# Rows through TensorE as transposes, and probabilities scaled on GpSimd ahead of their transposes, in a fused two-block transformer kernel

## What is computed

```
s_loc = q @ k.T * dh ** -0.5, -inf outside |i - j| <= 128
s_ctx = q @ k_c.T * dh ** -0.5
m     = max(max(s_loc), max(s_ctx), s_sink)
denom = sum(exp(s_loc - m)) + sum(exp(s_ctx - m)) + exp(s_sink - m)
o     = (exp(s_loc - m) @ v + exp(s_ctx - m) @ v_c) / denom
```

## Time and profile before

| what | value |
|---|---|
| median of 3 runs | 1319.2 us (1318.8 to 1322.29) |
| profiled execution | 1322.93 us |
| its span | 1320.9 us |
| TensorE matmul, busy | 1286.4 us, 97% of the span |
| VectorE busy | 896.2 us, 68% |
| ScalarE busy | 580.9 us, 44% |
| GpSimd busy | 109.9 us, 8% |

### The profile page before, as it was taken

How to read it: one execution, slowest core, us unless ns; L and a number is a source line. 1 busy time by engine, 2 the same in 40 slices (tenths; PEclk the granted TensorE clock), 3 DMA queues, 4 the chain that set the end, 5 groups by cost and what they waited for, 6 DMA issues and landing times.

```text
span 1320.9 us, 24297 instructions
## 1 busy us (share of the span) xinstructions
PE 1286.4 (97%) x10377; PEld 1196.9 (91%) x10377; DVE 896.2 (68%) x1387; ACT 580.9 (44%) x908; POOL 109.9 (8%) x161
## 2 busy tenths in 40 slices
PE   6999999999999999999999999999999999999997
PEld 4899999999998788999998998998999899899997
DVE  4577755576474564668587786786888986767567
ACT  4533355644774453534413213213165664535431
POOL 0111110000001111000000011110000210000000
PEclk9999999999999999999999999999999999999999
DMA  9997896545245453222445455575435102545550
GB/s 355 386 305 240 263 247 168 144 149 184 72 161 173 147 189 128 82 83 90 154 156 160 143 171 186 177 242 165 145 98 192 33 1 92 195 160 189 182 173 33
DMA packets 170152, 218.39 MB, mean 165 GB/s; under 512 B 6158, under 2 KB 147861, under 8 KB 169910
## 3 DMA queue, kind: packets, MB, share of 16 engines
q1 hardware_dynamic: 140196, 148.11, 34.4%
q0 software_dynamic: 29152, 67.42, 16.8%
q10 hardware_dynamic: 698, 1.32, 0.3%
HBM read 215.70 MB, written 1.12 MB: 164 GB/s over the span
## 4 chain that ended last, share of the span: by engine, by line
PE 87%; DVE 6%; ACT 2%; issue 2%; DMA 1%; SPq 1%; POOL 0%; DVEq 0%; ACTq 0%
PE bank L1353 31%; PE bank L705 12%; PE bank L724 11%; PE bank L757 7%; PE bank L740 4%; PE bank L1257 2%; PE bank L816 2%; PE bank L1331 1%; PE bank L903 1%; PE bank L1016 1%; PE bank L1431 1%; PE bank L1448 1%; PE bank L1499 1%; PE bank L1181 1%; DVE wlo L2151 1%
## 5 line engine op out<-in xcount | busy, mean ns | idle before, releaser
L2151 DVE TENSOR_TENSOR wlo<-raw,whi 128x2048 fp32r<-128x2048 f32 x131 | 297.3, 2274 | 90.2 <-ACT whi L1542 89.5
L1542 ACT ACTIVATE whi<-raw 128x2048 fp32r<-128x2048 f32 x131 | 248.0, 1899 | 187.0 <-PE bank L1353 133.2
L1353 PE MATMUL bank<-a_lo,whi 128*128 128x256 f32 (+1 forms) x688 | 166.4, 313 | 0.0
L1353 PE MATMUL bank<-whi,m_hi 128*128 128x256 f32 x576 | 162.5, 282 | 1.2 <-DVE m_lo L2757 0.8
L1353 PE MATMUL bank<-wlo,m_hi 128*128 128x256 f32 x576 | 161.8, 281 | 0.0
L1353 PE MATMUL bank<-whi,m_lo 128*128 128x256 f32 x576 | 161.7, 281 | 0.0
L1353 PEld LDWEIGHTS bank<-a_lo,whi 128*128 128x128 f32 x688 | 112.4, 188 | 8.9
L1353 PEld LDWEIGHTS bank<-whi,m_hi 128*128 128x128 f32 x576 | 110.0, 191 | 1.9 <-DVE m_lo L2757 1.2
L1353 PEld LDWEIGHTS bank<-whi,m_lo 128*128 128x128 f32 x576 | 109.3, 190 | 0.0
L1353 PEld LDWEIGHTS bank<-wlo,m_hi 128*128 128x128 f32 x576 | 109.1, 189 | 0.1
L705 PE MATMUL bank<-h_hi,whi 128*128 128x256 f32 x336 | 95.2, 283 | 0.0
(11 more groups left out here) (448 smaller groups left out, 3420.9 us busy)
## 6 DMA issues: line engine op xcount, KB each, us to landing
raw<-in_mlp_w SPq DMA_DIRECT2D x64, 1024.0 KB, 5.2
raw<-in_w_in SPq DMA_DIRECT2D x32, 1024.0 KB, 7.4
graw_b<-in_w_mod POOLq DMA_DIRECT2D x64, 512.0 KB, 4.8
raw<-in_ev_w_in SPq DMA_DIRECT2D x12, 1024.0 KB, 5.1
pre<-in_w_ada SPq DMA_DIRECT2D x16, 512.0 KB, 9.6
graw_a<-in_w_mod POOLq DMA_DIRECT2D x16, 512.0 KB, 7.0
Y<-in_w_mod POOLq DMA_DIRECT2D x16, 512.0 KB, 4.1
raw<-in_od_w_qkv SPq DMA_DIRECT2D x6, 1024.0 KB, 4.8
```

Source lines behind the costliest of these rows:

```text
L1353: mm = nc.tensor.matmul(o, x, y, start=(k == 0 and i == 0), stop=(k == KT - 1 and i == 2))
L1542: nc.scalar.activation(split_pair(u, kt * cols)[0], landing(u, kt * cols), ACT.Copy).then_inc(hi_done, 1)
L2151: nc.vector.tensor_tensor(split_pair(u, n)[1], landing(u, n), bf(whi[u % HI], n), ALU.subtract).then_inc(lo_done, 1)
```

## The change

Three things change.

1. `broadcast_row` and `gate_rows` use TensorE's transpose of the repeated column in place of a matmul by the identity.
2. In the attention GpSimd no longer builds `diag`. It multiplies the probabilities in place by the reciprocal, one 128x512 instruction per head, and `window_turn` transposes them plainly. `wa_n` now counts heads, so a head's transposes wait for its own scaling, and ScalarE's exp of a head waits for the transposes of the same head two pairs back.
3. VectorE does `window_sum(n-1)` ahead of `window_max(n)`, from n = 3 on.

```
-                if n >= 2:
-                    pool.wait_ge(wa_t, 2 * n - 2)
-                pool.tensor_tensor(diag[n % 2], spread(ident, [[0, 2], [1, P]]), spread(wst[:, n % 2, 6, :], [[1, 2], [0, P]]),
-                                   ALU.mult).then_inc(wa_n, 1)
+                for e in range(2):
+                    pool.tensor_tensor(prob1[2 * (n % 2) + e][:, 0:T], prob1[2 * (n % 2) + e][:, 0:T],
+                                       spread(wst[:, n % 2, 6, e:e + 1], [[0, T]]), ALU.mult).then_inc(wa_n, 1)
...
-                        mm = nc.tensor.matmul(bank[banks[2 * i + k // 4]][:, (k % 4) * P:(k % 4 + 1) * P],
-                                              spread(mod[:, c + k:c + k + 1], [[0, P]]), ident, start=True, stop=True)
+                        mm = nc.tensor.transpose(bank[banks[2 * i + k // 4]][:, (k % 4) * P:(k % 4 + 1) * P],
+                                                 spread(mod[:, c + k:c + k + 1], [[0, P]]), ident)
...
-                pe.wait_ge(wa_n, n + 1)
                 for e in range(2):
+                    pe.wait_ge(wa_n, 2 * n + e + 1)
                     if n:
                         pe.wait_ge(wa_lo, 2 * n - 1 + e)
                     else:
                         pe.wait_ge(kq_ev, KVH + 2)
                     for b in range(4):
-                        mm = nc.tensor.matmul(bank[6 + e][:, b * P:(b + 1) * P], prob1[2 * (n % 2) + e][:, b * P:(b + 1) * P],
-                                              diag[n % 2][:, e, :], start=True, stop=True)
+                        mm = nc.tensor.transpose(bank[6 + e][:, b * P:(b + 1) * P], prob1[2 * (n % 2) + e][:, b * P:(b + 1) * P], ident)
...
-                if n >= 2:
-                    act.wait_ge(wa_t, 2 * n - 2)
                 for e in range(2):
+                    if n >= 2:
+                        act.wait_ge(wa_t, 2 * n - 3 + e)
...
-                    dve.wait_ge(wa_n, n - 1)
+                    dve.wait_ge(wa_n, 2 * n - 2)
...
+                if 3 <= n <= PAIRS:
+                    window_sum(n - 1)
                 if n < PAIRS:
                     window_max(n)
                 if n < 2:
                     window_sum(n)
-                elif 3 <= n <= PAIRS:
-                    window_sum(n - 1)
```

More of the change, by code:

```diff
@@ L276, in build @@
             prob1.append(Y[:, 2, 0:T])
-            diag = [Y[:, 3, 2 * P * i:2 * P * (i + 1)].rearrange("p (e q) -> p e q", e=2) for i in range(2)]
         X_BANK = [bank[b] for b in (2, 2, 3, 3, 4, 4, 5, 5)]
@@ L787, in broadcast_row @@
                 for k in range(KT):
-                    mm = nc.tensor.matmul(bank[b0 + k // 4][:, (k % 4) * P:(k % 4 + 1) * P],
-                                          spread(col(k), [[0, P]]), ident, start=True, stop=True)
+                    mm = nc.tensor.transpose(bank[b0 + k // 4][:, (k % 4) * P:(k % 4 + 1) * P], spread(col(k), [[0, P]]), ident)
                 mm.then_inc(rowb, 1)
```

## The result

| | before | changed |
|---|---|---|
| median of 20 runs | 1321.2 us (1318.2 to 1325.45) | 1324.9 us (1322.44 to 1331.64) |
| profiled execution / its span | 1322.93 / 1320.9 us | 1323.96 / 1321.9 us |
| first maxima to output projection, from the traces | 1098.47 - 1020.15 = 78.32 us | 1102.50 - 1017.57 = 84.93 us |

The ratio of the changed kernel to the kernel before is **1.0033, 95% interval 1.0022 to 1.0043**: it is slower by 4.3 us (2.9 to 5.7). I had forecast 1327 us against a median of 1319.2, so +8; the direction and the place are right, the size is about twice what it is. The difference and the mechanism are what can be tested.

The account below looks back on a forecast made before the run. TensorE, busy for 97% of the span, was taken as the bound. Terms -4.5 - 4.3 + 17.3 gave +8.5 us, rounded to +8: 1327 us against a median of 1319.2, range 1309 to 1331.

Parts of the forecast that it names:

- a lock that holds both ways: Attention: VectorE's small two-SBUF-operand operations wait behind GpSimd's scalings, as GpSimd waited behind VectorE; chance 0.50.
- Part 4: GpSimd's wider scalings delay VectorE's small operations after the reductions by 1.15 us for each of 15 maxima: +17.3 us.
- Part 3: Attention stage without GpSimd's disturbance, sum ahead of maxima: steps averaging 3.78 us, gain nearly all in the tail, -4.3 us.
- Part 2: Attention turn: 8 plain transposes take 0.87 us per pair, TensorE's step falls from 4.30 to 3.46 us, no longer the bound.
- Part 1: Rows by single-instruction transposes save TensorE 0.90 us for each of five counted vectors: -4.5 us.
- Nobody disturbed: Rival: GpSimd's scalings do not delay VectorE's small operations in the attention; -8.8 us, 1310 us; chance 0.37.
- Half a lock: Rival: GpSimd is held off as often as VectorE, or ends at about 1.0 us; stall 0.4 to 0.7; chance 0.07.
- Two instructions: Rival: transposes of repeated columns or probabilities cost two instructions each, so rows and turn gain nothing; near 1336 us; chance 0.03.
- The clock: Rival: TensorE's clock drops to 1.2 GHz in the attention, steps near 7 us, time over 1350 us; chance 0.03.
- break-even: Attention: the change loses if VectorE's stall per maxima exceeds 8.8 / 15 = 0.59 us.

Follow-up runs that it names:

- two columns: Changed kernel, but GpSimd multiplies only the first 2 of 512 columns of each head's probabilities, the rest left unscaled; ratio to before 0.9945, 7.3 us faster.
- rows alone: Kernel before with only the rows made by TensorE transposes, attention left as it was; ratio to before 0.9973, 3.6 us faster.
- 384 columns: Changed kernel, but GpSimd multiplies only 384 of 512 columns of each head's probabilities, the last quarter left unscaled; ratio to before 0.9994.
- order alone: Kernel before with only VectorE's sum of n-1 moved ahead of the maxima of n; ratio to before 1.0011.

## Why the prediction was right, and where it was off

- *The mechanism*, a lock that holds both ways, is right. The prediction named L2873 or L2875, 0.7 us or more; L2873 has 0.90. Two of its other signs missed: GpSimd's instructions at 1.1 to 1.25 us (they last 1.04) and steps of 4.7 to 5.1 us (4.29 and 4.68).
- *Part 4, +17.3 us, is the term that was mis-sized*: it measures 10.45 (15 times 0.70 in place of 1.15). Two steps of it failed. I took 1.18 us for a scaling from the upper bound, twice the 0.61 of 256 columns. It lasts 1.04, and the second starts 1.00 after the first, so GpSimd is done at 2.28 us instead of 2.61 after the reciprocal's start: 0.3 us per step. With 2, 384 and 512 columns at 0.19, 0.83 and 1.04 us the fixed part is large, about 0.19 us, and doubling counts it twice. And I let the blocked operation *start* at GpSimd's end, or slip in between and hold L2879; in fact it ends there (L2875 starts at 2.34 us, where I had 2.72 to 2.81). That is the rest, 0.05 to 0.14 us.
- *Part 3, -4.3 us without a disturbance*: the stage is 3.8 us shorter with two columns, and the steps of 3.56 and, with `window_out`, 3.94 (I had 4.01) are as worked out from pair 0. The half microsecond that is missing lies in maxima 3 to 9: I put them at nothing, and they take 29.0 us against 28.1 before (the other terms came out 0.4 better together).
- *Part 2*: 8 transposes in place of 16 instructions per pair, and TensorE off the bound, as costed.
- *Part 1, -4.5 us*: about 2.7 measured, the 3.6 of the rows alone without the 0.9 that part 3 has. "All between matmuls that follow without a wait" is the step that failed: ahead of the matmuls behind two of the five vectors the work on VectorE that they need was done only 0.35 us before TensorE came.
- *The sum.* With the measured terms, -2.7 - 3.8 + 10.45 = +4.0 us, against a measured +4.3 (2.9 to 5.7). The forecast's error is part 4's 6.9 us too many, less 2.3 that parts 1 and 3 gave too much.
- *The rivals.* "Nobody disturbed" had -8.8 us, 1310: the kernel with two columns measures -7.3 (-10.0 to -4.6), 1314.0, so its sum is borne out within the interval and only the condition was false. "Half a lock" named two conditions. GpSimd is not held off as often as VectorE (its 32 scalings last 1.03 to 1.04 us), but its instructions do end at about 1.0 us, and with a stall of 0.70 this rival's sizes came nearer than the forecast's; its time of 1316 to 1321 did not. "Two instructions": the transposes are single. "The clock": it did fall, to half for 13.6 us of the attention, but the steady steps are 4.3 and 4.7 us and not 7, and the time is not over 1350. The break-even was given as 0.59 us per maxima; by the measured terms it is (2.7 + 3.8) / 15 = 0.43. 0.70 loses a little, and 384 columns with 0.31 do not lose (0.9994). The sign of the change hung on less than 0.3 us per step.

## What to carry to other kernels

When work moves to GpSimd, write down what SBUF tensors VectorE reads while it runs: here a VectorE operation on two numbers per partition, with two SBUF tensors, stood until the reading GpSimd instruction was over (0.90 us in place of 0.16), and if it is the last link ahead of another engine the whole ring waits. Place GpSimd's reads under VectorE work that reads PSUM, by a wait on GpSimd if need be. And "no wait behind it" says nothing about how much can be gained: look how long before TensorE's arrival the thing it needs was ready.

## What the runs showed that I had not expected

- GpSimd's multiplication by a repeated scalar takes 0.19, 0.61, 0.83 and 1.04 us for 2, 256, 384 and 512 columns (the 256 are `diag`'s, two heads of 128).
- A `tensor_scalar` of one column with a per-partition scalar lasts 0.21 us on VectorE, a two-tensor operation of two columns 0.16.
- TensorE's clock: the kernel before keeps it at full in the attention. With the changed kernel it is at half for 10.2 us from 1027 and for 3.4 us from 1061.6, and in the kernels with transposes in the turn for 3.4 to 6.8 us. The two kernels that keep `diag` (rows alone, order alone) stay at full there. It cost little: the step from 1062.52, most of it at half clock, is 4.29 us like the others. TensorE's waits and the plain transposes come together in all of these kernels; which of the two brings the clock down was not tried.
- The two profiled executions of before and after differ by 1.0 us, though the attention alone is 6.6 longer. At the start of the output projection the changed one is 4.0 us late, and between 1158 and 1201 (times of the kernel before) it makes up 3.0 of them, in a stage that the change doesn't touch. Before has TensorE at half clock for 3.4 us there (from 1159.5), which explains 1.7; the rest comes in pieces of 0.3 us per weight unit, with matmuls of 256 columns 0.113 or 0.118 us apart. The kernel with the rows alone shows the same pieces, from 660 on as well. What chooses between the two distances stays open; it can be one source of the 7 us by which runs of the same kernel differ, which these traces, one per kernel, don't show.
